# Four squares added by DVE before one sum on PE, one chunk later, in a fused two-block kernel

## The reference

```
y = ssd_chunked(xs, dt, A, Bm, Cm)
y = y + d_skip[:, None] * xs
y = y * silu(z)                                  # (S, 8 groups, 512)
y = y * rsqrt(mean(y * y, axis=-1) + EPS)        # the mean is over the 512 channels of a group
y = y * ssm_norm_w
```

## Time and profile before

| | us |
|---|---|
| median of 3 runs | 3291.51 (3288.75 to 3292.99) |
| span of the profiled execution | 3294.7 |
| PE busy | 3212.9 (98%) |
| PEld busy | 2938.4 (89%) |
| DVE busy | 2286.1 (69%) |
| ACT busy | 1535.2 (47%) |

### The profile page before, as it was taken

One profiled execution on the slowest core, in us unless ns is written; L12 is line 12 of the kernel. 1 busy time (PEld: TensorE's weight loads), 2 busy tenths in 40 slices (PEclk: granted clock), 3 DMA queues, 4 the chain that ended last, 5 costly groups with the idle time before them and its releaser, 6 DMA issues.

```text
span 3294.7 us, 52303 instructions
## 1 busy us (share of the span) xinstructions
PE 3212.9 (98%) x22161; PEld 2938.4 (89%) x22161; DVE 2286.1 (69%) x2781; ACT 1535.2 (47%) x1557; POOL 0.2 (0%) x4
## 2 busy tenths in 40 slices
PE   6999999999999999999999999999999999999999
PEld 4888989988999898988888888899899999999987
DVE  5798568887877878777776565776555665555676
ACT  2233565644555344433333333476665574433433
POOL 0000000000000000000000000000000000000000
PEclk9999999999999999999999999999999999999999
DMA  9897555566554776566665566544533444455554
GB/s 368 328 351 268 195 191 195 193 238 234 181 181 161 284 263 249 194 246 230 226 241 193 184 207 203 198 171 173 211 141 130 165 170 151 162 183 205 205 188 157
DMA packets 110413, 693.02 MB, mean 210 GB/s; under 512 B 11519, under 2 KB 18751, under 8 KB 36324
## 3 DMA queue, kind: packets, MB, share of 16 engines
q1 hardware_dynamic: 97776, 655.30, 54.9%
q10 hardware_dynamic: 12404, 34.38, 2.9%
HBM read 679.05 MB, written 13.72 MB: 210 GB/s over the span
## 4 chain that ended last, share of the span: by engine, by line
PE 83%; DVE 8%; DMA 3%; DVEq 2%; ACT 2%; issue 1%; ACTq 0%; SPq 0%
PE accp L511 26%; PE accp L512 14%; PE accp L516 11%; PE accp L517 11%; PE accp L518 11%; DVE wlo L1614 3%; DMA raw<-w 2%; PE accp L514 2%; ACT whi L1094 1%; DVE macc L1677 1%; DVEq L1679 1%; PE pw L592 1%; PE pw L1032 1%; PE pw L997 1%; DMA mraw_a<-wm 0%
## 5 line engine op out<-in xcount | busy, mean ns | idle before, releaser
L1614 DVE TENSOR_TENSOR wlo<-raw,whi 128x2048 fp32r<-128x2048 f32 (+1 forms) x544 | 1201.9, 2210 | 514.8 <-ACT whi L1094 509.5
L1094 ACT ACTIVATE whi<-raw 128x2048 fp32r<-128x2048 f32 (+1 forms) x544 | 1002.6, 1847 | 616.9 <-DMA raw<-w 588.0
L511 PE MATMUL accp<-act,whi 128*128 128x512 f32 x2550 | 908.9, 399 | 2.0 <-DVE tf L2144 1.0
L516 PE MATMUL accp<-act,whi 128*128 128x256 f32 x2912 | 840.9, 289 | 10.7 <-DVE wlo L1614 4.5
L517 PE MATMUL accp<-act,whi 128*128 128x256 f32 x2912 | 824.9, 283 | 0.0
L518 PE MATMUL accp<-act,wlo 128*128 128x256 f32 x2912 | 824.8, 283 | 0.0
L512 PE MATMUL accp<-act,wlo 128*128 128x256 f32 x2720 | 734.8, 280 | 0.0
L511 PEld LDWEIGHTS accp<-act,whi 128*128 128x128 f32 x2550 | 478.9, 188 | 112.7 <-DVE tf L2144 1.5
L516 PEld LDWEIGHTS accp<-act,whi 128*128 128x128 f32 x2912 | 559.4, 192 | 19.9 <-issue 7.9
L517 PEld LDWEIGHTS accp<-act,whi 128*128 128x128 f32 x2912 | 559.6, 192 | 5.2 <-issue 5.0
L518 PEld LDWEIGHTS accp<-act,wlo 128*128 128x128 f32 x2912 | 559.5, 192 | 0.0
(11 more groups left out here) (507 smaller groups left out, 4188.7 us busy)
## 6 DMA issues: line engine op xcount, KB each, us to landing
raw<-w SPq DMA_DIRECT2D x480, 1024.0 KB, 4.8
raw<-w SPq DMA_DIRECT2D x64, 704.0 KB, 4.1
mraw_a<-wm SPq DMA_DIRECT2D x42, 1024.0 KB, 7.5
mraw_b<-wm SPq DMA_DIRECT2D x16, 1024.0 KB, 8.4
mraw_c<-wm SPq DMA_DIRECT2D x16, 1024.0 KB, 6.9
mraw_x<-wm SPq DMA_DIRECT2D x10, 1024.0 KB, 14.9
acb<-ac_d ACTq DMA_DIRECT2D x8, 1024.0 KB, 4.7
mraw_w<-wm SPq DMA_DIRECT2D x8, 1024.0 KB, 6.9
```

The lines of the kernel that those rows point to most:

```text
L511: pe.matmul(acc, wh, both, start=first, stop=False, skip_group_check=True)
L516: pe.matmul(acc[:, 0:S], wh, x2[:, 0, :], start=first, stop=False)
L1094: act.activation(whi[:, c % 4, 0:k, :], raw[:, c % 4, 0:k, :], ACT.Copy).then_inc(hi_done, 1)
L1614: dve.tensor_tensor(wlo[:, c % 4, 0:k, :], raw[:, c % 4, 0:k, :], whi[:, c % 4, 0:k, :].bitcast(F32), ALU.subtract).then_inc(lo_done, 1)
```

## The change

In groups 0, 1 and 2 of each half (six of eight) the four squares are added on DVE at the end of the group: one instruction adds tiles 2 and 3 onto tiles 0 and 1 (512 elements per partition), a drain, and one adds tile 1 onto tile 0 (256 elements). PE then waits for `sq_sum` and sums over partitions with one matmul instead of four. This matmul is moved from chunk 0 of the next group, ahead of k = 12, to chunk 1, ahead of k = 3. `ssq_mm` now counts once per group instead of four times. The last group of a half keeps its four matmuls and its place.

```diff
             def squares_summed(g):

+                if g % 4 < 3:
+                    pe.wait_ge(sq_sum, deferred(g))
+                    pe.matmul(pw[:, 5, 0:S], ones[:, :], sq4(0), start=True, stop=True).then_inc(ssq_mm, 1)
+                    return
                 for t in range(4):
                     pe.wait_ge(sq_ok, 4 * g + t + 1)
-                    pe.matmul(pw[:, 5, 0:S], ones[:, :], sq4(t), start=t == 0, stop=t == 3).then_inc(ssq_mm, 1)
+                    mm = pe.matmul(pw[:, 5, 0:S], ones[:, :], sq4(t), start=t == 0, stop=t == 3)
+                mm.then_inc(ssq_mm, 1)
...
                 def opening_rhs(k):
-                    if k == 12:
+                    if k == 3:
                         squares_summed(g - 1)
                     return act2[:, k]

                 for j in range(10):
-                    chunk(C0[ph] + 10 * gg + j + 20 * i, E0[ph] + 10 * gg + j + 20 * i, opening_rhs if g % 4 and j == 0 else acts)
+                    chunk(C0[ph] + 10 * gg + j + 20 * i, E0[ph] + 10 * gg + j + 20 * i, opening_rhs if g % 4 and j == 1 else acts)
...
# ACT, j == 2
-                            act.wait_ge(ssq_mm, 4 * g)
+                            act.wait_ge(ssq_mm, g)
...
# DVE
             def norm_sums(g):

                 v = xdd[:, 0:S]
-                dve.wait_ge(ssq_mm, 4 * g + 4)
+                dve.wait_ge(ssq_mm, g + 1)
...
                 split_lo(C0[ph] + 10 * gg + 11 + 20 * i)
+                if g % 4 < 3:
+                    dve.wait_ge(sq_ok, 4 * g + 4)
+                    dve.tensor_tensor(dec[:, 0:4:2, :, :], dec[:, 0:4:2, :, :], dec[:, 4:8:2, :, :], ALU.add)
+                    dve.drain()
+                    dve.tensor_tensor(sq4(0), sq4(0), sq4(1), ALU.add).then_inc(sq_sum, 1)
                 if g % 4 == 3:
                     norm_sums(g)
                     norm_scale(g)
```

More of the change, by code:

```diff
@@ L301, in first_and_second_block @@
         y_mm, y_ev, sq_ok = sem("y_mm"), sem("y_ev"), sem("sq_ok")
+        sq_sum = sem("squares_added")
         ssq_mm, ssq_v, ssq_r, grp = sem("ssq_mm"), sem("ssq_v"), sem("ssq_r"), sem("grp_done")
```

## The result

| | kernel before | changed kernel |
|---|---|---|
| median of 20 runs each, us | 3291.1 (3287.6 to 3297.5) | 3295.6 (3292.1 to 3298.8) |
| ratio to before | | 1.0015, 95% interval 1.0009 to 1.0021 |
| the same again, 11 runs of the changed kernel | 3290.6 (27 runs) | 3296.8, ratio 1.0016 (1.0007 to 1.0025) |
| span of the profiled execution | 3294.7 | 3295.5 |

A forecast was written before the change was run, and what follows sets the result against it. DVE's chain from the sum of squares was taken to bound the groups: moved 2.46 us later, less 1.28 us removed, additions free, gives +1.18 us in six groups, +7.1 us, 3298.6 us; likeliest 3296 to 3302, range 3289 to 3305.

The forecast's parts named there:

- The bound: State space groups opening with a deferred norm: DVE's 47.87 us from the sum to xdd sets the loop, 64.04 us a group.
- The rival that PE is the bound: State space groups: PE's work sets the time, so all 7.7 us saved are won, 3283.8 us; chance 0.14.
- the draw by a shorter chain: DVE's chain in each group loses its 0.74 us wait for ACT's copy, 2.6 us slower in all, 3294.1; chance 0.12.
- Removed and moved: PE's sum of squares: three of four matmuls go, 1.28 us; start 2.46 us later; sum 1.18 us later, at +7.45 us.
- Added: DVE's two additions at group end, 0.69 and 0.43 us, end at about +5.3 us in idle time; price 0.
- The sum: State matmul L781 at +55.38 us instead of +54.20, 1.18 us later in each of six groups, +7.1 us.
- Where the pauses fall: PE first pauses at chunk 4, 1.8 us, shown as 1.65; the rest at chunk 7 and L781.
- The first rival: New PE pauses at chunk 4 each bring a stretch of lower clock, 6 us more, 3304.7 us; chance 0.08.
- The chances: Whole execution: slower 0.53, same 0.33, faster 0.14; about 0.2%, 6.6 us, is what can be told from no change.

The follow-up runs named there:

- e1: Kernel before with its four matmuls of squares, unchanged in number, moved to chunk 1 ahead of k = 3; 3306.6 us, ratio 1.0046.
- e2: Changed kernel with its one matmul back at chunk 0, k = 12, and DVE's additions left out; 3282.3 us, ratio 0.9972 to the kernel before.
- e3: Changed kernel without DVE's additions, PE waiting for ACT's squares instead; 3294.9 us, ratio 1.0011 to the kernel before.
- e5: Changed kernel with norm_sums on DVE moved behind convolve(0); 3301.3 us, ratio 1.0036 to the kernel before.
- e6: Kernel before with norm_sums on DVE moved behind convolve(0); 3313.5 us, ratio 1.0072.

## Why the prediction was right

**The bound.** "The loop is set by DVE with nothing to spare" is shown. e1 moved a sum and nothing else and lost 14.8 us in the stage, e2 shortened it and won 7.8 us; PE's work is the same in e1 as before. The rival that PE is the bound would have given 0 for e1 and 7.7 us faster for the change, and is out: PE had the highest busy share, and still did not set the group. So is the draw by a shorter chain: the changed kernel's chain is 47.84 to 47.93 us in five of six groups, and the wait for ACT's copy is 0.82 us, not less than before.

**Removed and moved.** The sum came at +7.45 us to the hundredth, 1.18 us later, and e1 (2.47 us a group) and e2 (1.30 us) confirm the two terms of it apart, 2.46 and 1.28 us. L787 came at +55.37 us, forecast +55.38: the 0.1 to 0.3 us that a new pause might cost PE beyond its own length did not appear.

**Added.** The additions took 0.68 and 0.42 us, ended at +5.17 us (about +5.3 forecast), and e3 shows their price of 0.

**The sum.** 7.1 us forecast for the stage, 7.0 us measured there (6.8 when repeated). The first group rose by 0.81 us only: its DVE chain went from 48.21 to 47.84 us, while the second group's went from 47.87 to 48.20 us and that group rose by 1.52 us. A stretch of 0.35 us in the chain fell into another group; the sum did not change. The whole execution shows 4.9 us (3.0 to 6.9), less than the stage. The prediction let nothing change outside the stage, and that was its one wrong size: the parts named with the two kernels' second profiles are together about 2.7 us shorter in the changed kernel and those made from it, where the whole lacks 2.1 us against the stage (1.5 us in the second comparison). Why they are is not shown. The second comparison (1.0007 to 1.0025) gives 5.3 us, 2.3 to 8.2.

**Where the pauses fall** was partly wrong. I put the first pause at chunk 4, 1.65 us of idle time. The profile shows it in two parts, 0.44 us ahead of L772, which waits for ACT's SiLU of the second tile, and 1.13 us at chunk 4. I had not looked at that wait, which depends on the same DVE chain. The pause as a whole was right: chunk 4 started at +25.43 us (659.05 - 633.62), forecast +25.44. The rest of PE's delay falls into small holds at later chunks, each too short to show as idle time, and one of 0.2 us ahead of L787.

**The clock.** The first rival did not come: the clock is 1.00 over the whole stage. In the changed kernel no pause reached 1.65 us, but two of the experiments test the rival. e5 has pauses of 1.39 to 1.74 us ahead of L772, and e6 has five of 1.65 to 1.67 us and one of 2.01 us:

```profile
954.86 0.71 PE L766 MATMUL pw<-bct 128*128 128x128 f32 x4 [2.01 <-ACT bct L1276]
```

The windows behind that last one, 954.86 to 956.86 and 956 to 958, show 1.00, and so does the whole stage of e6. The pause of 1.95 us that the prediction feared was followed by 0.57, so the length of one pause alone does not decide it; what does is not shown here.

**The chances.** With 4.9 us out of 3291, 0.15%, the measured ratio clears 1 but lies under the 0.2% that I took as the line to "no change". So by my own line the outcome is the one to which I gave 0.33, not the "slower" with 0.53. The mechanism and the direction were right, and the middle of the forecast, 7.1 us, is 1.4 times what the whole execution shows.

## What to carry to other kernels

Where two engines hand the path to each other once per iteration, find the instruction at which it changes hands (the idle time of the one ends there, and it works without a gap from there on). What stands ahead of it counts in full, by its length and by its place: here a step of k of delay cost 0.35 us a group and a matmul removed won 0.43 us, though PE showed 100% busy. Read the gain or loss of a stage from the stage: here the whole execution showed 2 us less, while parts far behind the stage moved as well. Before an instruction is moved ahead of such a wait, follow the results that other engines need from the work behind it: e5 took away a 2.3 us wait and got one of the same length from the engine between.

## What the runs showed of the hardware that was not expected

The trace records an f32 matmul of 128x256 as two passes of 0.214 us on PE, 0.43 us in all. The changed kernel bears this out: from the start of the sum to the next matmul of the low part are 1.95 us with four matmuls (572.47 to 574.42) and 0.66 us with one (640.44 to 641.10), 1.29 us for three. One of the same size with rounded inputs takes 0.12 us, the step from L518 to the next matmul.

Holds of PE of 0.06 to 0.2 us at a handover did not show as idle time, because the recorded busy time of a matmul reaches past the start of the next one: 0.28 us recorded against a step of 0.12 us for L518, thus 0.16 us. The wait was only to be seen by comparing starts.

PE pauses of 1.65 to 2.01 us in the state space stage (e6) left the granted clock at 1.00, while one of 1.95 us in a later stage was followed by 0.57.
